# One program per engine for two stages of a diffusion block, with the heads' buffers laid over the front stage's

## The chip, the core and the metric

The kernel runs on one core of one Trainium2 chip. A core has four compute engines, TensorE (PE, matrix products), VectorE (DVE), ScalarE (ACT) and GpSimd (POOL), and a sync engine (SP) that here only issues DMAs. Each engine runs its own list of instructions, and they meet only through semaphores. The metric is the device time of one execution in microseconds (us).

## The reference, cut to what matters

One layer (DEPTH is 1) of a diffusion backbone over 2048 latent tokens and 256 context tokens of width 1024:

```python
shift, scale, gate = split(silu(c) @ w_ada + b_ada, 3)            # also from c_ctx for the context tokens
hc = rmsnorm(ctx) * (1 + scale_c) + shift_c                       # (256, 1024)
hx = rmsnorm(x + sincos) * (1 + scale) + shift                    # (2048, 1024)
s_f, s_b = final_state(hc @ w_in[:, :3072])                       # one 128x128 state per head and direction
i_in, z_f, z_b, q_in, gate_a, u_f, gate_f = split(hx @ w_in)      # 7 pieces of 1024 columns
k = (1 - lb) * sigmoid(-z);  log_f = log(max(1 - k, 1e-6))        # 8 heads of 128, forward and backward
o = chunk_scan(silu(q), k_f, v, log_f, s_f) + flip(chunk_scan(...backward...))
y_a = rmsnorm_per_head(o) * silu(gate_a)
y_f = (real 2-D Fourier mix of u_f, 4 groups) @ w_fourier * silu(gate_f)
out = rmsnorm(x + gate * (concat(y_a, y_f) @ w_out))
```

## The kernel before

Three stages follow each other, each a function: `front`, `heads` and `tail`. Products are made in three passes, of high and low parts of both factors (`mm3`, L60 to L62), so each product costs three matmuls.

**front** (0 to 617 us) makes the hidden rows and holds them in SBUF as 4 groups of 512 tokens (`h_hi`, `h_lo`). It then multiplies them with blocks of 256 weight columns: the value columns (kind 0, four blocks) and the columns of `gate_a` (kind 1, four blocks), eight fills of 256 tokens each (`rows_fill`), which ScalarE evacuates and stores to DRAM. Among the fills stand, for each head, `context_forget` (forget gates of the context), `turn_key` and `context_state`; VectorE's `weigh` lies between the first two. `residual_gate(j)` makes a quarter of the row `gate`. Last comes head 0: `context_forget(0)` and the 12 products `first_unit`, which give head 0 its keys (forward, backward) and its query, since the heads stage computes these only for the next head. Each weight block is loaded to `raw` by SyncE and split by VectorE in `split_block`; `HOME` says in which of two homes the parts lie, `block_a(n)` and `block_c(h)` give the number of the block of gate columns n or of head h's forget columns.

**heads** (617 to 1985 us) runs 8 heads of 4 steps. A step (L987 on) takes 512 tokens in both directions: TensorE makes the scores level by level, VectorE prepares the next step's operands (`prepare`, `first_operands`), and between these TensorE computes ten half products (`project_half`) of 12 matmuls for columns that the next head or the tail needs. Their weights come from GpSimd's DMA into `head_raw`, are split by ScalarE (high part, L1064) and VectorE (low part, L1126).

**tail** (1991 us to the end) does the Fourier mix, the output product and the last norm.

What sets the order is the program text of each stage. Every stage is a `nc.Block()` of its own: it starts when all engines have met at a barrier and ends with another. Its buffers and semaphores belong to a `Room`. When a room is left, a further block in which only GpSimd works clears the room's semaphores one by one (L100), and `heads` has one more block before it, `start_at_one` (L127), that adds one to each of its semaphores but one. GpSimd's list has 72 clears behind front, 32 behind heads and 86 behind tail. Because front's room is closed before heads' is opened, heads' first loads, its memsets and the split of its first weights all come behind front's last store and these blocks.

Of the kernel before, what the change touches and what calls it, by code (L numbers as in the profile page):

```python
# [22 lines left out]

# [11 lines left out]
P = 128  # L35
# [29 lines left out]
def after(n):  # L65

    return n + 1


# [11 lines left out]
class Room:  # L83

    def __init__(self, nc, stage):
        self.nc, self.stage, self.stack, self.sems, self.at_one = nc, stage, ExitStack(), [], []
# [29 lines left out]
    def sem(self, name, from_zero=False):  # L118
        s = self.stack.enter_context(self.nc.semaphore(f"{self.stage}_{name}"))
        self.sems.append(s)  # L120
        if not from_zero:
            self.at_one.append(s)
        return s

    def start_at_one(self):

        with self.nc.Block() as block:  # L127

            @block.gpsimd
            def _(pool):  # L130
                for s in self.at_one:
                    pool.sem_inc(s, 1)


# [18 lines left out]
def front(nc, x_rows, ctx_rows, w_ada, w_in, conds, b_ada, b_ada_cols, norm_w_cols, bounds_cols, row_codes, col_code, masks_in,  # L153
          ident, masks, one_minus_lb, h_base, h_hi, h_lo, states, value_rows, gate_rows_a, pieces, gate_row):

# [9 lines left out]
    BLOCKS = 17  # L165

# [10 lines left out]
    HOME = (0, 1, 0, 0, 1, 1, 0, 0, 1, 1, 0, 0, 1, 1, 0, 0, 1)  # L177

    def fill_of(kind, n, f):
        return (KT + 1) * n + f if kind == 0 else (KT + 1) * NB + KT * n + f  # L180

    FIRST_FILL = (KT + 1) * NB + KT * NB

    def store_of(kind, n, f):
        return KT * (NB * kind + n) + f

    FIRST_STORE = 2 * KT * NB
# [3 lines left out]
    with Room(nc, "front") as r:  # L191
        hc_base = r.slab("hc", 2 * HC)
        hc_hi, hc_lo = r.at("hc_hi", [P, KT, CTX], hc_base, F32R), r.at("hc_lo", [P, KT, CTX], hc_base + HC, F32R)
        work = r.slab("work", 61440)
        raw = r.at("raw", [P, KT, W], work)
# [1065 lines left out]

# [802 lines left out]
```

## Time and profile before

| | us |
|---|---|
| median of 3 runs | 2613.98 (2613.46 to 2616.17) |
| the profiled execution | 2614.39 |
| its span, first to last instruction | 2612.5 |
| TensorE busy | 2472.2 (95% of the span) |
| VectorE busy | 1446.9 (55%) |
| ScalarE busy | 504.9 (19%) |
| mean granted TensorE clock | 0.972 |

The profiled execution is 1.9 us longer than its span, and 0.4 us over the median. Busy time says how much an engine worked; a wait says which event ended its idle time. TensorE is busy for 95% of the span, so what is left between its matmuls is small and lies at few places. Clock 1.00 means 2.4 GHz and 0.50 means 1.2 GHz.

### The profile page before, as it was taken

How to read it: one execution, taken by the hardware profiler on the slowest of the kernel's cores; microseconds unless marked ns; L12 is line 12 of the kernel's file. 1: busy time of each engine (PE TensorE's matmuls, PEld its weight loads, DVE VectorE, ACT ScalarE, POOL GpSimd, SP SyncE). 2: the span in 40 equal slices, each digit the busy share in tenths (PEclk: the TensorE clock that was granted, in tenths of full speed). 3: DMA queues.
4: the chain of work that ended last, by engine and by line, in shares of the span. 5: the costliest groups of instructions: out<-in, count | busy, mean ns of one | idle time of the engine just before them, and what ended most of it. 6: DMA issues, size and time to landing. Idle time of an engine off the chain costs nothing. (4 is left out here: it accounts for less than half of the span.)

```text
span 2612.5 us, 38225 instructions
## 1 busy us (share of the span) xinstructions
PE 2472.2 (95%) x15856; PEld 2134.5 (82%) x15856; DVE 1446.9 (55%) x2984; ACT 504.9 (19%) x775; POOL 44.0 (2%) x64
## 2 busy tenths in 40 slices
PE   7899999995999999999999999999995999799997
PEld 3799999994888888888888888888884787688885
DVE  4712121111676767666666666666785675555553
ACT  3611111110111112111111111111111333222221
POOL 0000000000000000000000000000000001000000
PEclk9899999997999999999999999999997999899999
DMA  8332233213223232323233232323224336344341
GB/s 292 109 91 68 83 97 98 88 53 91 68 86 109 88 101 84 109 79 114 91 104 93 91 106 86 105 88 109 72 89 171 123 148 234 134 157 152 130 175 55
DMA packets 215646, 288.90 MB, mean 111 GB/s; under 512 B 13609, under 2 KB 146865, under 8 KB 211890
## 3 DMA queue, kind: packets, MB, share of 16 engines
q1 hardware_dynamic: 128114, 173.33, 20.1%
q10 hardware_dynamic: 79728, 85.34, 9.4%
q0 software_dynamic: 7632, 27.79, 3.6%
q8 instruction: 126, 2.06, 0.3%
q14 instruction: 46, 0.38, 0.0%
HBM read 193.08 MB, written 93.33 MB: 110 GB/s over the span
## 5 line engine op out<-in xcount | busy, mean ns | idle before, releaser
L60 PE MATMUL head_ps_proj<-hidden_h_hi,head_hi 128*128 128x512 f32 x1184 | 487.9, 412 | 25.4 <-DVE head_lo L1126 25.4
L62 PE MATMUL head_ps_proj<-hidden_h_hi,head_lo 128*128 128x512 f32 x1184 | 465.0, 393 | 0.0
L61 PE MATMUL head_ps_proj<-hidden_h_lo,head_hi 128*128 128x512 f32 x1184 | 463.6, 392 | 0.0
L60 PE MATMUL front_bank<-front_hi,hidden_h_hi 128*128 128x256 f32 x1024 | 294.9, 288 | 6.2 <-DVE hidden_h_lo L364 6.2
L62 PE MATMUL front_bank<-front_hi,hidden_h_lo 128*128 128x256 f32 x1024 | 291.5, 285 | 0.0
L61 PE MATMUL front_bank<-front_lo,hidden_h_hi 128*128 128x256 f32 x1024 | 291.5, 285 | 0.0
L1080 ACT ACTIVATE head_projected<-head_ps_proj 128x512 f32<-128x512 f32 x148 | 88.5, 598 | 1003.1 <-PE head_ps_proj L62 1003.1
L60 PEld LDWEIGHTS head_ps_proj<-hidden_h_hi,head_hi 128*128 128x128 f32 x1184 | 224.3, 189 | 68.0 <-issue 25.7
L62 PEld LDWEIGHTS head_ps_proj<-hidden_h_hi,head_lo 128*128 128x128 f32 x1184 | 223.6, 189 | 50.1
L61 PEld LDWEIGHTS head_ps_proj<-hidden_h_lo,head_hi 128*128 128x128 f32 x1184 | 224.6, 190 | 39.6
L60 PEld LDWEIGHTS front_bank<-front_hi,hidden_h_hi 128*128 128x128 f32 x1024 | 198.4, 194 | 11.4 <-DVE hidden_h_lo L364 9.4
L1209 DVE TENSOR_TENSOR head_query<-head_query,head_total 128x256 f32<-128x256 f32 x256 | 108.4, 423 | 172.5 <-PE head_ps L1011 119.0
L61 PEld LDWEIGHTS front_bank<-front_lo,hidden_h_hi 128*128 128x128 f32 x1024 | 198.4, 194 | 0.0
L62 PEld LDWEIGHTS front_bank<-front_hi,hidden_h_lo 128*128 128x128 f32 x1024 | 198.3, 194 | 0.0
L1171 DVE RECIPROCAL head_inverse<-head_gate 128x448 f32<-128x448 f32 x64 | 186.1, 2932 | 0.0
L1011 PEld LDWEIGHTS head_ps<-head_query,head_key 128*128 128x128 f32 x1024 | 124.9, 193 | 6.6 <-DVE head_key L1210 1.1
L1011 PE MATMUL head_ps<-head_query,head_key 128*128 128x64 f32 x1024 | 122.4, 273 | 1.5 <-DVE head_key L1210 1.0
L1194 DVE TENSOR_TENSOR head_query<-head_query,head_gate 128x512 f32<-128x512 f32 x64 | 44.3, 693 | 142.0 <-PE head_ps L998 142.0
L60 PE MATMUL tail_bank<-tail_w_hi,tail_a_hi 128*128 128x512 f32 x256 | 104.2, 407 | 7.3 <-DVE tail_a_lo L1619 7.3
L1145 DVE COPY_PREDICATED head_score<-hidden_masks,head_ps 128x512 f32<-128x512 uint8 (+1 forms) x192 | 109.1, 621 | 0.0
L1046 PE MATMUL head_ps<-head_value,head_score 128*128 128x128 f32 x512 | 99.6, 276 | 10.0 <-DVE head_state L1240 10.0
L998 PE MATMUL head_ps<-head_query,head_first_half 128*128 128x64 f32 x512 | 100.5, 279 | 7.7 <-DVE head_key L1185 7.7
(213 smaller groups left out, 4322.3 us busy)
## 6 DMA issues: line engine op xcount, KB each, us to landing
head_raw<-in_w_in POOLq DMA_DIRECT2D x37, 512.0 KB, 5.1
head_query<-piece_query SPq DMA_DIRECT2D x64, 256.0 KB, 5.3
head_value<-value_rows SPq DMA_DIRECT2D x64, 256.0 KB, 6.4
head_out<-head_o ACTq DMA_DIRECT2D x64, 256.0 KB, 4.7
tail_o<-head_out SPq DMA_DIRECT2D x32, 512.0 KB, 5.9
front_raw<-in_w_in SPq DMA_DIRECT2D x17, 512.0 KB, 4.7
front_w_mod<-in_w_ada SPq DMA_DIRECT2D x8, 1024.0 KB, 14.0
front_stage<-in_x SPq DMA_DIRECT2D x16, 512.0 KB, 8.5
```

Source lines behind the costliest of these rows:

```text
L60: nc.tensor.matmul(out, st_hi, mv_hi, start=start, stop=False)
L61: nc.tensor.matmul(out, st_hi, mv_lo, start=False, stop=False)
L62: return nc.tensor.matmul(out, st_lo, mv_hi, start=False, stop=stop)
L998: done = nc.tensor.matmul(half_block(ps[d][0][:, t, :], d, half), tile(keys, t), half_block(tile(query[d][b], t), d, half), start=True, st ...
L1011: done = nc.tensor.matmul(meeting(ps[d][BANK_OF[i]][:, t, :], d, LEVELS[i]), tile(key[d][b], t), meeting(tile(query[d][b], t), d, LEVELS[i ...
L1046: nc.tensor.matmul(ps[d][2][:, t, :], score[d][:, t, :], value[d][b][:, t, :], start=True, stop=False)
L1080: nc.scalar.activation(projected[unit % 2][:], ps_proj[unit % 2][:], PIECES[name][1], scale=PIECES[name][2]).then_inc(proj_copied, 1)
L1145: nc.vector.copy_predicated(dst, mask.to_broadcast(list(dst.shape)), src).then_inc(copied[d], 1)
L1171: nc.vector.reciprocal(in_blocks(inverse[d][:], d)[:, :, 1:BASE], in_blocks(gate[d][:], d)[:, :, 1:BASE]).then_inc(gated[d], 1)
L1194: nc.vector.tensor_tensor(qs, qs, f[:, :, 0:1].to_broadcast([P, GRP // BASE, BASE]), ALU.mult)
L1209: nc.vector.tensor_tensor(qs[:, :, 1, :], qs[:, :, 1, :], tot[:, :, 0, :].to_broadcast(shape), ALU.mult)
```

## The change

Front and heads become one block, so that each engine goes on from its last front instruction to its first heads instruction without a barrier; what heads needs is passed as semaphores with counts (`Handover`), and waited for one by one at the first use. The heads' buffers are laid at fixed offsets in front's work area, over buffers that are spent by then, and the eight PSUM banks are shared. The fourth block of gate columns, with its residual gate, moves behind head 0's pieces, and head 7's context work is put between and ahead of these. `start_at_one` goes (a wait for a count of zero is left out instead), and the clears move: front's 72 into heads at head 2, heads' 33 to the beginning of the tail, 40 of the tail's 86 into the tail, with 46 left in a block at the end. No product and no ScalarE or VectorE arithmetic of the steps is changed. VectorE makes one cast more and two memsets fewer, ScalarE one copy and two table loads fewer.

```diff
 class Room:
     def __exit__(self, failed, *a):
-        if self.sems and not failed:
-            with self.nc.Block() as block:
-                @block.gpsimd
-                def _(pool):
-                    for s in self.sems:
-                        pool.sem_clear(s)
         self.stack.close()
+    def clear(self, pool, but=()):
+        kept = [s.num for s in but]
+        for s in self.sems:
+            if s.num not in kept:
+                pool.sem_clear(s)
-    def start_at_one(self):
-        with self.nc.Block() as block:
...
 # front: numbers of the weight blocks, fills and stores
     def block_c(h):
-        return 15 if h == 0 else 2 * h
+        return 14 if h == 0 else 13 if h == 7 else 2 * h
     def block_a(n):
-        return 7 + 2 * n
-    BLOCK_Q = 16
+        return 16 if n == NB - 1 else 7 + 2 * n
+    BLOCK_Q = 15
...
 # front, SyncE
-            for n in range(NB):
+            for n in range(NB - 1):
                 load_block(COL_GA + n * W, block_a(n))
                 load_gate(n)
                 sp.wait_ge(gate_row_done, n + 1)
                 load_forget(NB + n)
                 store_gate(n)
+            load_forget(HEADS - 1)
             load_forget(0)
             sp.wait_ge(lo_done, BLOCK_Q)
             sp.dma_start(raw[:, :, 0:P], w_view[:, :, COL_Q:COL_Q + P]).then_inc(w_here, DMA)
-            sp.wait_ge(gate_out, NB * DMA)
-            sp.wait_ge(masks_in_sem, DMA)
+            load_block(COL_GA + (NB - 1) * W, block_a(NB - 1))
+            load_gate(NB - 1)
+            store_gate(NB - 1)
 # front, VectorE, after the loop over the gate blocks
-            split_block(block_c(0), 28)
-            v.wait_ge(product, fill_of(1, NB - 1, KT - 1) + 1)
-            split_block(BLOCK_Q, 29, P)
+            split_block(block_c(HEADS - 1), 24)
+            v.wait_ge(product, fill_of(1, NB - 2, KT - 1) + 1)
+            split_block(block_c(0), 26)
+            weigh(HEADS - 1)
+            v.wait_ge(z_done, HEADS - 1)
+            split_block(BLOCK_Q, 27, P)
             weigh(0)
+            v.wait_ge(product, FIRST_FILL + 2 * NG)
+            split_block(block_a(NB - 1), 28)
+            add_gate_bias(NB - 1)
 # front, TensorE, after the loop over the gate blocks (ScalarE's list is moved alike)
+            context_forget(HEADS - 1)
+            for unit in range(2):
+                first_unit(block_c(0), 0, unit)
+            turn_key(HEADS - 1)
+            first_unit(block_c(0), 0, 2)
+            context_state(HEADS - 1)
+            first_unit(block_c(0), 0, 3)
             context_forget(0)
-            for unit in range(NG):
-                first_unit(block_c(0), 0, unit)
+            for unit in range(NG, NG + 2):
+                first_unit(block_c(0), P, unit)
             turn_key(0)
-            first_unit(block_c(0), P, NG)
+            first_unit(block_c(0), P, NG + 2)
             context_state(0)
-            for unit in range(NG + 1, 2 * NG):
-                first_unit(block_c(0), P, unit)
+            first_unit(block_c(0), P, NG + 3)
             for unit in range(2 * NG, 3 * NG):
                 first_unit(BLOCK_Q, 0, unit)
+            residual_gate(NB - 1)
+            for f in range(KT):
+                rows_fill(1, NB - 1, f)
 # heads: buffers at fixed places in front's work slab, banks shared with front
-    with Room(nc, "head") as r:
-        raw = r.sb("raw", [P, KT, P])
-        hi = [r.sb(f"hi{b}", [P, KT, P], F32R) for b in range(2)]
+    HC, VALUES, QUERY_W, RAW, GATE_W, OUT_ROWS, LITTLE = (work + i * KB for i in (60, 44, 28, 0, 8, 24, 76))
+    raw = r.at("raw", [P, KT, P], HC)
+    hi = [r.at(f"hi{b}", [P, KT, P], at, F32R) for b, at in enumerate((HC + 2 * row, GATE_W))]
...
+    ps_proj = bank[4:6]
+    ps = [[by_tile[6 + d], by_tile[d], by_tile[2 + d]] for d in range(2)]
 # heads, GpSimd
-                for d in range(2):
-                    pool.memset(score[d][:], 0.0).then_inc(cleared, 1)
-                    pool.memset(first_half[d][:], 0.0).then_inc(cleared, 1)
+        pool.wait_ge(handed.z_done, HEADS)
+        name, head = pieces(0, False)[0]
+        pool.dma_start(raw[:], w_view[:, :, bass.ds(PIECES[name][0] + head * P, P)]).then_inc(w_here, DMA)
+        pool.wait_ge(handed.product, handed.first_fills)
+        for d in range(2):
+            pool.memset(first_half[d][:], 0.0).then_inc(near_cleared, 1)
+        pool.wait_ge(handed.product, handed.all_fills)
+        pool.wait_ge(handed.gate_out, N_BLOCKS * DMA)
+        for d in range(2):
+            pool.memset(score[d][:], 0.0).then_inc(score_cleared, 1)
+        turn(0, False, first=1)
...
+            if h == 2:
+                for d in range(2):
+                    pool.wait_ge(product[d], PROD * NG * h)
+                    pool.wait_ge(o_stored[d], NG * h * DMA)
+                front_room.clear(pool)
 # heads, SyncE
+        def first_loads():
+            for o_stage in range(2):
+                sp.wait_ge(handed.stored[o_stage], handed.keys_stored)
+            sp.wait_ge(handed.z_done, HEADS)
+            sp.wait_ge(handed.s_done, HEADS)
+            load(0, 0, ("key", "value"))
+            for o_stage in range(2):
+                sp.wait_ge(handed.stored[o_stage], handed.queries_stored)
+            sp.wait_ge(handed.s_out, HEADS * 2 * DMA)
+            load(0, 0, ("query",))
+            sp.wait_ge(handed.product, handed.first_fills)
+            start_state(0)
+            sp.wait_ge(handed.gate_row_done, N_BLOCKS)
+            load(0, 1, ("key", "query"))
+            sp.wait_ge(handed.product, handed.all_fills)
+            load(0, 1, ("value",))
 # heads, TensorE
+            if n == 0:
+                pe.wait_ge(handed.evacuated, handed.all_fills)
...
-                pe.wait_ge(cleared, 7)
+        pe.wait_ge(handed.sig_done, HEADS)
+        pe.wait_ge(handed.gate_added, N_BLOCKS)
+        pe.wait_ge(handed.key_t_copied, HEADS)
+        pe.wait_ge(handed.s_copied, HEADS)
 # heads, VectorE
-                for d in range(2):
-                    nc.vector.memset(ps[d][2][:], 0.0).then_inc(cleared, 1)
-                v.wait_ge(cleared, 7)
+        v.wait_ge(w_here, DMA)
+        nc.vector.tensor_copy(hi[0][:], raw[:]).then_inc(hi_done, 1)
         split_low(0, 0)
+        v.wait_ge(handed.s_done, HEADS)
         for part in range(GATED + 1):
             prepare(0, 0, part)
+        v.wait_ge(near_cleared, 2)
         first_operands(0, 0)
 # tail, GpSimd, and after its block
                 pool.memset(eps[:], EPS).then_inc(eps_set, 1)
+                heads_room.clear(pool)
...
+                pool.wait_ge(out_stored[1], 2 * DMA)
+                r.clear(pool, but=LATE)
+        with nc.Block() as block:
+            @block.gpsimd
+            def _(pool):
+                for sem in LATE:
+                    pool.sem_clear(sem)
 # program
-            front(nc, x[0], ctx[0], w_ada, w_in, conds, b_ada, b_ada_cols, norm_w_cols, bounds_cols, row_codes, col_code, masks_in,
-            heads(nc, w_in, one_minus_lb, ident, masks, h_hi, h_lo, states, value_rows, pieces, o_rows)
...
+            work = s.slab("work", WORK)
+            bank = [s.ps(f"bank{i}") for i in range(8)]
+            with nc.Block() as block:
+                handed = front(nc, block, front_room, work, bank, x[0], ctx[0], w_ada, w_in, conds, b_ada, b_ada_cols, norm_w_cols,
...
+                heads(nc, block, heads_room, front_room, work, bank, handed, w_in, one_minus_lb, ident, masks, h_hi, h_lo, states,
```

TensorE at the passage from front to heads, before (`front_bank` is a front product, `head_ps_proj` the first half product of heads):

```order
L60 MATMUL front_bank<-hidden_h_hi_52,front_hi_61 128x512
L61 MATMUL front_bank<-hidden_h_lo_56,front_hi_61 128x512
L62 MATMUL front_bank<-hidden_h_hi_52,front_lo_63 128x512
L264 UNCONDITIONAL_BRANCH
L963 UNCONDITIONAL_BRANCH [waits barrier_Pool_Activation_PE_DVE_SP_release]
L60 MATMUL head_ps_proj<-hidden_h_hi_49,head_hi 128x512 [waits head_proj_copied,head_lo_done,head_cleared]
```

The same place in the changed kernel (the products ahead are now of the last gate columns, 256 wide):

```order
L61 MATMUL hidden_bank<-front_hi_61,hidden_h_hi_52 128x256
L62 MATMUL hidden_bank<-front_lo_63,hidden_h_hi_52 128x256
L63 MATMUL hidden_bank<-front_hi_61,hidden_h_lo_56 128x256
L1040 UNCONDITIONAL_BRANCH
L61 MATMUL hidden_bank<-hidden_h_hi_49,head_hi_5978 128x512 [waits front_s_copied,front_key_t_copied,head_lo_done,front_gate_added,front_sig_done]
```

The barrier is gone; the first product of heads waits for the split of its weights and for four front events that lie eight fills back.

VectorE at the same passage, before (the first two rows end `weigh(0)`):

```order
L401 TENSOR_TENSOR front_key<-front_key,front_gate 128x255 [waits front_scan_done]
L402 TENSOR_TENSOR front_key<-front_key,front_gate 128x255
L264 UNCONDITIONAL_BRANCH
L1121 UNCONDITIONAL_BRANCH [waits barrier_Pool_Activation_PE_DVE_SP_release]
L1252 MEMSET head_ps 128x512 x2
L1126 TENSOR_TENSOR head_lo<-head_raw,head_hi 128x1024 [waits head_hi_done,head_cleared]
L1153 TENSOR_SCALAR head_key<-head_key,hidden_one_minus_lb 128x512 [waits head_loaded00]
```

and in the changed kernel:

```order
L406 TENSOR_TENSOR front_key<-front_key,front_gate 128x255
L384 CAST front_hi_61<-front_raw 128x2048 [waits front_w_here,front_product]
L386 TENSOR_TENSOR front_lo_63<-front_raw,front_hi_61 128x2048 [waits front_hi_done]
L411 TENSOR_TENSOR front_gate_part<-hidden_bank,front_gate_part 1x256 [waits front_gate_bias_in,front_gate_row_done]
L1205 UNCONDITIONAL_BRANCH
L1339 CAST head_hi_5978<-head_raw 128x1024 [waits head_w_here]
L1210 TENSOR_TENSOR head_lo_5980<-head_raw,head_hi_5978 128x1024 [waits head_hi_done]
L1237 TENSOR_SCALAR head_key_5988<-head_key_5988,hidden_one_minus_lb 128x512 [waits head_loaded00,front_s_done]
```

The split of the last gate block and the gate's bias stand ahead of the passage now, and the heads' first split and `prepare` follow them with no barrier.

GpSimd's list from front's end on, before (ISA rows are semaphore clears):

```order
L264 UNCONDITIONAL_BRANCH
L97 UNCONDITIONAL_BRANCH [waits barrier_Pool_Activation_PE_DVE_SP_gather]
L100 ISA x72
L95 UNCONDITIONAL_BRANCH
L129 UNCONDITIONAL_BRANCH [waits barrier_Pool_Activation_PE_DVE_SP_gather]
L127 UNCONDITIONAL_BRANCH
L912 UNCONDITIONAL_BRANCH [waits barrier_Pool_Activation_PE_DVE_SP_gather]
L915 MEMSET head_score 128x512
L916 MEMSET head_first_half 128x512
L915 MEMSET head_score 128x512
L916 MEMSET head_first_half 128x512
L921 DMA head_raw<-in_w_in 128x8x128 [waits head_lo_done] x37
```

and in the changed kernel:

```order
L952 UNCONDITIONAL_BRANCH
L961 DMA head_raw<-in_w_in 128x8x128 [waits front_z_done]
L964 MEMSET head_first_half_6000 128x512 [waits front_product]
L964 MEMSET head_first_half_6001 128x512
L968 MEMSET head_score_6008 128x512 [waits front_gate_out,front_product]
L968 MEMSET head_score_6009 128x512
L957 DMA head_raw<-in_w_in 128x8x128 [waits head_lo_done] x14
L93 ISA [waits head_product1,head_o_stored1,head_o_stored0,head_product0]
L93 ISA x71
L957 DMA head_raw<-in_w_in 128x8x128 [waits head_lo_done] x22
```

The 72 clears stand between two weight loads of the heads now, and the first weight load waits for front's last `context_forget` alone.

## Rows read from the trace of the kernel before

**Rows 1.** The longest waits, whole span: engine and line, releaser, total us, times, longest

```profile
PE head_ps_proj L60 <- DVE head_lo L1126: 25.4, 1, 25.4
PE tail_bank L1879 <- DMA tail_chan<-in_chan_tables: 11.5, 1, 11.5
```

**Rows 2.** Timeline, TensorE, front's end to step 1: start us, us, line, tiles, count

```profile
617.11 0.39 PE L62 MATMUL front_bank<-hidden_h_hi,front_lo 128*128 128x512 f32 x1
642.85 0.76 PE L60 MATMUL head_ps_proj<-hidden_h_hi,head_hi 128*128 128x512 f32 x1 [25.35 <-DVE head_lo L1126]
...
654.43 0.66 PE L998 MATMUL head_ps<-head_query,head_first_half 128*128 128x64 f32 x2 [6.13 <-DVE head_key L1185]
...
699.75 0.48 PE L60 MATMUL head_ps_proj<-hidden_h_hi,head_hi 128*128 128x512 f32 x1
```

**Rows 3.** Timeline, TensorE, starts of steps 0 and 1 of head 1

```profile
829.04 0.50 PE L60 MATMUL head_ps_proj<-hidden_h_hi,head_hi 128*128 128x512 f32 x1
...
871.75 0.48 PE L60 MATMUL head_ps_proj<-hidden_h_hi,head_hi 128*128 128x512 f32 x1
```

**Rows 4.** Windows: from:to, us, busy PE, PEld, DVE, ACT, POOL, then PEclk, DMA share

```profile
617.50:642.80 25.30, 0.00 (x0) 0.00 (x0) 2.24 (x4) 1.65 (x2) 2.90 (x5) 0.58 0.52 150
642.80:660.00 17.20, 11.02 (x38) 9.39 (x39) 14.57 (x29) 0.00 (x0) 0.96 (x1) 0.60 0.17 46
...
828.90:871.60 42.70, 42.70 (x289) 36.96 (x288) 32.30 (x86) 8.56 (x12) 1.76 (x2) 1.00 0.34 105
```

**Rows 5.** Timeline, the other engines between front and step 0

```profile
612.10 0.60 ACT L540 ACTIVATE front_out<-front_bank 128x512 f32<-128x512 f32 x1 [4.84 <-PE front_bank L62]
...
617.54 0.60 ACT L540 ACTIVATE front_out<-front_bank 128x512 f32<-128x512 f32 x1 [4.84 <-PE front_bank L62]
618.16 0.33 ACTq L542 DMA_DIRECT2D piece_query<-front_out  x1
...
629.39 0.53 POOL L915 MEMSET head_score<- 128x512 f32 x1 [627.93 <-POOLq L127]
...
641.53 1.22 DVE L1126 TENSOR_TENSOR head_lo<-head_raw,head_hi 128x1024 fp32r<-128x1024 f32 x1 [10.93 <-ACT head_hi L1064]
```

**Rows 6.** DMA by issue line and queue, 617 to 643 us: count, KB, us to landing

```profile
q14 instruction: 1, 0.01, 0.1%
...
head_value<-value_rows SPq DMA_DIRECT2D x4, 256.0 KB, 8.5
...
piece_query<-front_out ACTq DMA_DIRECT2D x1, 256.0 KB, 2.4
```

**Rows 7.** Timeline, TensorE and VectorE, work that is moved in front

```profile
431.18 3.62 PE L711 MATMUL front_bank<-front_raw,front_silu 128*2 128x256 f32 x16
...
457.86 0.28 PE L60 MATMUL front_bank<-front_hc_hi,front_hi 128*128 128x256 f32 x1
...
463.62 0.28 PE L60 MATMUL front_bank<-front_hi,hidden_h_hi 128*128 128x256 f32 x1
...
464.45 0.62 DVE L390 TENSOR_SCALAR front_key<-front_key,hidden_one_minus_lb 128x256 f32<-128x256 f32 x2 [20.53 <-ACT front_key L548]
...
469.27 2.29 DVE L382 TENSOR_TENSOR front_lo<-front_raw,front_hi 128x2048 fp32r<-128x2048 f32 x1
...
487.09 1.06 PE L703 MATMUL front_bank<-front_v_ctx,front_key_t 128*128 128x128 f32 x8
```

**Rows 8.** Timeline, the last stores of heads and tail, and tail's start

```profile
1984.61 0.99 ACTq L1105 DMA_DIRECT2D head_out<-head_o  x2
1991.13 0.40 ACTq L1797 DMA_DIRECT2D tail_hn<-in_hgrn_cols  x1
...
2603.10 0.34 ACTq L1795 DMA_DIRECT2D out<-tail_x  x1
```

**Rows 9.** DMA by issue line, around these two stores

```profile
head_out<-head_o ACTq DMA_DIRECT2D x2, 256.0 KB, 2.5
...
out<-tail_x ACTq DMA_DIRECT2D x1, 512.0 KB, 2.6
```

More of the change, by code:

```diff
@@ L22 @@
 from contextlib import ExitStack
+from dataclasses import dataclass
 import concourse.bass as bass
@@ L150, with front @@
 N_BLOCKS = HG // W
-def front(nc, x_rows, ctx_rows, w_ada, w_in, conds, b_ada, b_ada_cols, norm_w_cols, bounds_cols, row_codes, col_code, masks_in,
+KB = 1024
+WORK = 78 * KB
+@dataclass
+class Handover:
+    z_done: object
+    sig_done: object
+    key_t_copied: object
+    s_done: object
+    s_copied: object
+    s_out: object
+    gate_row_done: object
+    gate_added: object
+    gate_out: object
+    product: object
+    evacuated: object
+    stored: list
+    masks_in: object
+    first_fills: int
+    all_fills: int
+    keys_stored: int
+    queries_stored: int
+    all_stored: int
+def front(nc, block, r, work, bank, x_rows, ctx_rows, w_ada, w_in, conds, b_ada, b_ada_cols, norm_w_cols, bounds_cols, row_codes, col_code, masks_in,
           ident, masks, one_minus_lb, h_base, h_hi, h_lo, states, value_rows, gate_rows_a, pieces, gate_row):
@@ new lines, in front @@
+    stage0 = [r.at(f"stage{b}", [P, D], work + 28672 + 4096 * b) for b in range(4)]
+    TMP = 3
+    tmp = [r.at(f"tmp{i}", [P, GRP], work + 45056 + 2048 * i) for i in range(TMP)]
+    col = r.at("col", [P, H], work + 51200)
+    junk = r.at("junk", [P, D], work + 53248)
+    v_ctx = r.at("v_ctx", [P, CT, HG], work + 45056)
+    key = r.at("key", [P, 2, CTX], work + 53248)
+    gate = r.at("gate", [P, 2, CTX], work + 55296)
+    key_t = r.at("key_t", [P, 2, CT, P], work + 57344)
+    state = r.at("state", [P, 2, P], work + 59392)
@@ new lines, in heads @@
+    inverse = [piece(f"inverse{d}", VALUES + (4 + d) * row) for d in range(2)]
+    first_half = [piece(f"first_half{d}", QUERY_W + (1 + d) * row) for d in range(2)]
+    key_t = [tiles(f"key_t{d}", QUERY_W + (3 + d) * row) for d in range(2)]
+    state = [r.at(f"state{d}", [P, TPG + 1, P], QUERY_W + 5 * row + d * (TPG + 1) * P * 4) for d in range(2)]
+    total = [r.at(f"total{d}", [P, 2 * GRP // BASE], QUERY_W + 15 * KB + d * KB // 2) for d in range(2)]
+    score = [tiles(f"score{d}", at) for d, at in enumerate((GATE_W + 7 * row, LITTLE))]
@@ L1296, in tail @@
     H = D // 2
-    KB = 1024
     F_FIRST = 6
@@ L2007, in program @@
     y_f = scratch("fourier_out", (FW, SEQ))
-    with Room(nc, "all") as r:
+    with Room(nc, "all") as r, Room(nc, "head") as heads_room:
         ident = r.sb("ident", [P, P])
-        with Room(nc, "hidden") as s:
+        with Room(nc, "hidden") as s, Room(nc, "front") as front_room:
             masks = s.sb("masks", [P, 2, MASKED, P], U8)
```

1869 lines of the change are left out of this document (935 added, 934 removed).

## The prediction, made before the changed kernel was run

> **What bounds the kernel now.** I read the busy shares first: TensorE 95%, VectorE 55%. So TensorE bounds the kernel, and only what stands between its matmuls, or slows them, can be won. The list of waits comes next. The longest single idle time of TensorE is the passage from front to heads, 25.4 us, and after it the start of the tail, 11.5 us [rows 1]. The chain of waits says nothing on the first: it is followed back only to 1991 us, where all engines leave a barrier together. So the timeline and the windows must carry the argument.
>
> The timeline shows the whole price of the passage [rows 2]. The last front matmul starts at 617.11 us; matmuls of this shape follow each other at 0.23 us, so without the passage the next would start at 617.34. The first of heads starts at 642.85: 25.51 us lost. Step 0 then runs until step 1 starts at 699.75, which is 56.90 us. The same step of head 1, with the same work, takes from 829.04 to 871.75, 42.71 us [rows 3]. So step 0 loses 14.19 us more. Of these, 6.13 are a wait for VectorE's first operands [rows 2]; the other 8.06 go to the clock. After the idle time the granted clock is 0.60 in the window of 17 us in which step 0 begins, while it is 1.00 in the undisturbed step [rows 4]; 0.50 is the lower level, 1.2 GHz.
>
> The other engines' timeline says what the 25 us consist of [rows 5]. ScalarE's last store is issued at 618.16 and lands 2.4 us later [rows 6], at 620.56. The first heads instructions start at 629.39, after 72 clears, 31 increments and three barriers. Then GpSimd's weights, ScalarE's split and VectorE's split (641.53) follow one after another, all with TensorE idle.
>
> **Part 1: the passage.** TensorE's work is the same: the eight fills of the last gate block and one residual gate go behind the twelve products of head 0, and context work of head 7 goes ahead. If nobody makes TensorE wait, front still ends at 617.34 and step 0 follows at once, 42.71 us long. Whether it waits is a matter of when the others are ready, so I place them on before's times.
>
> Eight fills are 384 matmuls at 0.12 us (48 matmuls from 457.86 to 463.62 are 5.76 us [rows 7]), 46.1 us, and the residual gate takes 3.6 [rows 7]. So head 0's query is done at 617.3 - 46.1 - 3.6 = 567.6, and its keys four products of 5.44 us [rows 5] earlier, at 545.9.
> - VectorE splits the gate block after the keys (a cast of about 1.2 us, then 2.29 [rows 7]): 549.4. The residual gate's weights may then be loaded; even at the 8.5 us of the slowest load in the passage [rows 6] they are there at 558, before 567.6.
> - VectorE adds the gate's bias at about 571.6. SyncE stores it, and then issues the keys and values of step 0, and the queries, whose store was issued at about 568.2 and has landed by 571. With six issues of about 0.5 us and 8.5 us to land [rows 6], all is there by 583.
> - VectorE's path from its first split to the first operands is 641.53 to 654.43, 12.9 us [rows 2, 5], at its own pace, since it waits there for no matmul. Its cast in ScalarE's place adds about 1 us. So operands stand at 597, when TensorE still has 20 us of fills. The low part of the weights is ready at 574.
> - GpSimd clears `first_half` at 568 and `score` from 617.3 on, two memsets of 0.53 us [rows 5]. VectorE first uses `score` only after step 0's first scores, some 8 us into the step.
> - The values of step 1 wait for the last fill too: 617.3 + 8.5 = 626; in head 1, VectorE takes up the next step's keys 15 us into the step.
>
> Further ahead, the tightest place is where the forget columns of head 0 are split. VectorE must wait for the end of gate block 2 (487.09 [rows 7]) and needs 3.5 us: 490.6. TensorE meanwhile does a context state, 1.06 us, and `context_forget(7)`, 5.76 us [rows 7], and wants them at 493.9. The margin is 3.3 us. `weigh(7)` and `weigh(0)` have two products, 10.9 us, as cover; VectorE takes from 464.45 to about 468.0 for one, the cast of a block ahead of 469.27 taken off [rows 7], so 3.6 us.
>
> The branch that is left on TensorE between the stages has no row. Its cost lies between 0 and what two barriers with their branches cost, 1.4 us (worked out below); I take 0, since the branches in before sit inside those barriers. The page Runtime: NRT & Kernel Launch of the Trainium skill (Instruction fetch mechanics) warns that a taken branch whose target is not yet fetched stalls the engine for a fetch; by the time of a small DMA that would add about 2 us. The trace speaks against it here: from 617 to 643 us, with two such branches on each engine, the view of the queues lists one instruction packet in all [rows 6].
>
> Part 1 saves 25.51 + 14.19 = 39.70 us. Bounds: if all idle time and slow clock goes, 39.7; if only the barriers and clears go (629.39 - 620.56), 8.8.
>
> **Part 2: clears and barriers elsewhere.** Clears have no rows, but three stretches hold them. Behind heads: the second store is issued about 0.6 us after 1984.61 and lands 2.5 us later, at 1987.7; the tail starts at 1991.13 [rows 8, 9]. That is 3.4 us for 32 clears and two barriers. Behind the tail: issued at 2603.10, landed after 2.6 us at 2605.7, end of the span 2612.5, so 6.8 us for 86 clears and two barriers [rows 8, 9]. The difference, 3.4 us for 54 clears, gives 0.062 us for one and 1.4 us for two barriers. The third stretch tests it: 103 x 0.062 + 3 x 0.7 = 8.5 us, where 8.8 were measured.
> - Behind heads 32 clears and one barrier go: 2.0 + 0.7 = 2.7 us. The 33 clears lie at the tail's beginning on GpSimd, whose first other work there comes after the folds, far later. Bounds 0 and 3.4.
> - At the end 40 clears go: 2.5 us. They run inside the tail, where GpSimd is done. Bounds 0 and 6.8.
> - Front's 72 clears in head 2 hold GpSimd for 4.5 us between two weight loads. Those weights are used a good part of a head later. Cost nothing; without that cover 4.5 us.
> - The tail's first wait, 11.5 us, gets shorter by the 2.7 us already counted, and stays over 8 us, so I leave the lower clock behind it as it is.
>
> **The sum.** 39.7 + 2.7 + 2.5 = 44.9 us, from 2614.39 gives 2569.5. The profiled execution is 0.4 over the median of the runs, less than I can tell, so 2569.5 stands for the median too.
>
> **Rivals.**
> - A new wait at the passage. VectorE's or SyncE's chain comes over 20 us later than I place it, for instance because SyncE, blocked at the gate's bias, issues the loads late and one wait of 5 us opens before the first scores. Then the clock falls as well and costs up to the 8.1 us above: 2569.5 + 5 + 8 = 2582.5. For it: every one of these loads now stands behind the gate's store in SyncE's list. Against: 20 us of slack, on durations that the trace has.
> - A small hole, up to 3 us, at the split of head 0's columns (3.3 us of margin), or a stalled branch: 2572. By the skill's rule above it would be 2571.5, which is this rival too.
> - Clears and barriers don't get cheaper, since the landing of the last store and a fixed time behind it set both ends: 2614.4 - 39.7 = 2574.7. For it: no row shows a clear. Against: three stretches fit one price.
> - The change doesn't do what it says: TensorE's first heads product still waits for something that comes at the very end of front, and only the 8.8 us of barriers are saved there: 2614.4 - 8.8 - 5.2 = 2600.4.
> - Slower. In every step of the heads, a buffer or bank that now has another place makes TensorE wait for VectorE, where before the two were just in time. VectorE is busy 32.3 of 42.7 us in a step [rows 4], so some 10 us of lag must be used up at one point. With 32 steps it decides from 44.9 / 32 = 1.4 us a step on; at 1.6 us a step the kernel takes 2569.5 + 51 = 2620.7. Against: no instruction or wait of a step is changed but for the first.
>
> **How the numbers follow.** My forecast 0.74, with 2567 to 2572.5 as its own range; the small hole 0.07; clears at their old price 0.05; new wait 0.08; nothing hidden 0.03; slower 0.02; about as before, from a mixture of the last two, 0.01. What a measurement can tell from no change is 0.2%, 5.2 us. All but the last two cases lie more than that below before: faster 0.97, same 0.01, slower 0.02. The range runs from 2565, for steps that gain a little at the tail's start, to 2579, which takes in the small hole, the clears, and the shorter new waits.
>
> **What would show it.** In the changed profile: TensorE's longest wait at the passage under 1 us; granted clock 1.00 through it; step 0 about 42.7 us; front's last matmul at 617 us still, with no wait of TensorE between 480 and 617; VectorE idle for some 20 us before step 0's first scores; the tail's first DMA about 2.7 us sooner after the last heads store; the span ending about 4.3 us after the last store lands instead of 6.8; the steps of later heads as long as before. A wait of TensorE for `head_lo` or `head_key`, a window with a clock under 1.00 around 620 us, or a longer step would prove me wrong.

## The result, and the profile after

The changed kernel takes 2566.51 us (median of 4 runs, 2565.05 to 2569.57), the kernel before 2613.72 (4 runs, 2612.65 to 2616.17). The ratio is 0.982, with an interval from 0.9803 to 0.9837: 47.2 us less. The forecast was 2569.5, in a range from 2565 to 2579. The span of the profiled execution is 2563.3 us, 49.2 less than before.

The timeline of TensorE in the changed kernel shows the passage from front to heads (columns as in [rows 2]):

```profile
615.08 0.28 PE L63 MATMUL hidden_bank<-front_hi,hidden_h_lo 128*128 128x256 f32 x1
615.20 0.40 PE L61 MATMUL hidden_bank<-hidden_h_hi,head_hi 128*128 128x512 f32 x1
...
657.75 0.48 PE L61 MATMUL hidden_bank<-hidden_h_hi,head_hi 128*128 128x512 f32 x1
```

The last product of front and the first of heads are 0.12 us apart, where [rows 2] have 25.74. Step 0 lasts from 615.20 to 657.75, 42.55 us, where it was 56.90. The windows that answer to [rows 4] have TensorE busy throughout, at the full clock:

```profile
617.50:642.80 25.30, 25.30 (x185) 21.70 (x184) 17.26 (x48) 2.85 (x4) 0.88 (x1) 1.00 0.31 97
642.80:660.00 17.20, 17.20 (x106) 15.24 (x105) 11.72 (x26) 5.70 (x8) 0.00 (x0) 1.00 0.13 38
```

The other engines' timeline answers to [rows 5]. The rows of VectorE and SyncE say how early step 0 was ready:

```profile
565.63 0.98 POOL L964 MEMSET head_first_half<- 128x512 f32 x2 [43.63 <-PE hidden_bank L63]
...
569.14 0.41 DVE L411 TENSOR_TENSOR front_gate_part<-hidden_bank,front_gate_part 1x256 f32<-1x256 f32 x1 [21.75 <-PE hidden_bank L726]
...
569.58 0.24 SPq L309 DMA_DIRECT2D residual_gate<-front_gate_part  x1
570.00 0.36 SPq L992 DMA_DIRECT2D head_key<-piece_key_f  x1
...
590.10 0.42 DVE L1269 TENSOR_TENSOR head_key<-head_key,head_inverse 128x256 f32<-128x256 f32 x1
...
619.88 0.69 DVE L1278 TENSOR_TENSOR head_query<-head_query,head_gate 128x512 f32<-128x512 f32 x1 [29.35 <-PE hidden_bank L1075]
```

SyncE issues the first heads load at 570.00, behind the gate's store. The first operands stand at 590.5. TensorE asks for them at 617.95, so 27 us were in hand. VectorE then sits idle for 29.35 us until the first scores: slack that was on TensorE before is on VectorE now, where it costs nothing.

The two other borders, which answer to [rows 8], are the last store of heads with the tail's first instruction, and the last store of all (the span ends at 2563.3):

```profile
1940.38 0.99 ACTq L1190 DMA_DIRECT2D head_out<-head_o  x2
1944.09 0.40 ACTq L1884 DMA_DIRECT2D tail_hn<-in_hgrn_cols  x1
...
2556.66 0.34 ACTq L1882 DMA_DIRECT2D out<-tail_x  x1
```

The first distance falls from 6.52 to 3.71 us, the second (2603.10 to 2612.5 before) from 9.40 to 6.64. Of TensorE's longest waits the one for `head_lo` is gone, and the one for the tail's channel tables is shorter (line, releaser, total us, times, longest; 11.5 before [rows 1]):

```profile
PE tail_bank L61 <- DVE tail_fold_lo L1628: 11.1, 1, 11.1
...
PE tail_bank L1966 <- DMA tail_chan<-in_chan_tables: 8.1, 1, 8.1
...
PE tail_bank L1975 <- DVE tail_once L1618: 6.0, 1, 6.0
```

So the span's 49.2 us come from the passage (39.86), the border behind heads (2.81), the end (2.76), and 3.8 us that no part of the change aims at. About 2.1 of these lie in front's first 130 us, and 2.2 at the start of the last head; the tail, from its first instruction to its last store, is 0.6 us longer. From the start of step 1 of head 0 to the first scores of the last head both kernels take 1162.9 us. At the start of the last head both kernels wait 1.58 us for VectorE ahead of the first scores. Before, the clock falls behind this wait; in the changed kernel it doesn't (before first, then changed: the wait, then a window over the end of these scores):

```profile
1862.70 0.41 PE L998 MATMUL head_ps<-head_query,head_first_half 128*128 128x64 f32 x2 [1.58 <-DVE head_key L1185]
...
1866.00:1870.00 4.00, 4.00 (x17) 0.50 1.01 328
```

```profile
1820.69 0.41 PE L1075 MATMUL hidden_bank<-head_query,head_first_half 128*128 128x64 f32 x2 [1.58 <-DVE head_key L1269]
...
1824.00:1828.00 4.00, 4.00 (x25) 1.00 1.05 349
```

Both differences are looked at behind the experiments.

### The profile page after: what moved, and what is told of

The parts are those of the page before. It is cut to its first block and busy times, and to the rows that moved or that the text cites. A ratio compares the mean times of both kernels' runs of the same rounds, so it can differ in the third digit from the quotient of the medians.

```text
span 2563.3 us, 38144 instructions
## 1 busy us (share of the span) xinstructions
PE 2461.8 (96%) x15856; PEld 2126.8 (83%) x15856; DVE 1447.1 (56%) x2983; ACT 501.2 (20%) x772; POOL 44.0 (2%) x64
## 5 line engine op out<-in xcount | busy, mean ns | idle before, releaser
L61 PE MATMUL hidden_bank<-hidden_h_hi,head_hi 128*128 128x512 f32 x1184 | 485.3, 410 | 0.0
L63 PE MATMUL hidden_bank<-hidden_h_hi,head_lo 128*128 128x512 f32 x1184 | 463.0, 391 | 0.0
L62 PE MATMUL hidden_bank<-hidden_h_lo,head_hi 128*128 128x512 f32 x1184 | 461.3, 390 | 0.0
L61 PE MATMUL hidden_bank<-front_hi,hidden_h_hi 128*128 128x256 f32 x1024 | 294.8, 288 | 6.2 <-DVE hidden_h_lo L368 6.2
L62 PE MATMUL hidden_bank<-front_lo,hidden_h_hi 128*128 128x256 f32 x1024 | 291.5, 285 | 0.0
L63 PE MATMUL hidden_bank<-front_hi,hidden_h_lo 128*128 128x256 f32 x1024 | 291.5, 285 | 0.0
L63 PEld LDWEIGHTS hidden_bank<-hidden_h_hi,head_lo 128*128 128x128 f32 x1184 | 222.2, 188 | 49.6
L61 PEld LDWEIGHTS hidden_bank<-hidden_h_hi,head_hi 128*128 128x128 f32 x1184 | 222.8, 188 | 41.8
L62 PEld LDWEIGHTS hidden_bank<-hidden_h_lo,head_hi 128*128 128x128 f32 x1184 | 223.2, 188 | 39.2
L61 PEld LDWEIGHTS hidden_bank<-front_hi,hidden_h_hi 128*128 128x128 f32 x1024 | 198.4, 194 | 11.4 <-DVE hidden_h_lo L368 9.4
```

The lines of the kernel that those rows point to most:

```text
L61: nc.tensor.matmul(out, st_hi, mv_hi, start=start, stop=False)
L62: nc.tensor.matmul(out, st_hi, mv_lo, start=False, stop=False)
L63: return nc.tensor.matmul(out, st_lo, mv_hi, start=False, stop=stop)
```

## Experiments

Theory: TensorE loses nothing at a border as long as every other engine can run over it ahead of TensorE. That needs two things at once: no barrier at the border, and TensorE work at front's end that doesn't feed step 0. Rivals: only the barriers and clears were dear, or only the order was; or the low clock has a cause of its own. Each kernel is the changed one with the edit shown, but for one, which starts from the kernel before. Its ratio is against the kernel before on the same chip.

### Two blocks

```diff
+            with nc.Block() as block:
                 heads(nc, block, heads_room, front_room, ...
```

> The changed kernel, but heads stand in a block of their own, so that the engines meet at a barrier between front and heads; the new order of the front, the buffers and the moved clears stay. My theory (the passage is gained because the engines run on over the border, so that head 0's loads, splits and first operands are made under the front's last products): TensorE is idle again for about 25.5 - 8 (104 clears and increments and their barriers are gone) = 17.5 us at the border, waits again for the second half of the operands (6.1) and runs step 0 at the low clock (8.1): 2566.5 + 31.7 = about 2598. Rival A (the order alone brings the gain, the border costs a barrier of 0.7 us): 2567 to 2569. Rival B (the low clock doesn't come back after a shorter gap): 2590.

Measured: 2594.75 us, 0.9932 [0.9917, 0.9947], 28.2 over the changed kernel. TensorE's waits between 600 and 660 us:

```profile
PE hidden_bank L61 <- DVE head_lo L1210: 11.7, 1, 11.7
PE hidden_bank L1075 <- DVE head_key L1269: 7.1, 1, 7.1
```

One line of code brings back 28 of the 47 us, so rival A falls, and rival B with it. Step 0 runs from 627.54 to 684.66, 57.12 us: 7.1 are the second wait and 7.5 the clock. The gap alone is smaller than I expected, 11.8 us against 17.5. GpSimd's first load is issued at 617.85, 2.3 us after the last front product, where the kernel before without its clears, below, needs 5.8. Of these 3.5 us some 2.0 lie at the barrier, and the rest in memsets that stand ahead of the load there. I read the first part as the barrier having less to wait for when front's last work doesn't feed heads; no run tests it alone.

### The old order in one program

```diff
-        for n in range(NB - 1):
+        for n in range(NB):
             residual_gate(n)
...
-        residual_gate(NB - 1)
-        for f in range(KT):
-            rows_fill(1, NB - 1, f)
```

(and the same on the other engines: head 0's query comes last again)

> The changed kernel as one program per engine, but with the kernel before's order in the front: the last gate columns' 8 fills stand ahead of head 0's pieces again, which come last. My theory: with the query's pieces last, their evacuation, store, load and split for step 0 can't lie beside TensorE's work: idle for about 20 us at the border, and then step 0 at the low clock (8 us more): 2566.5 + 28 = about 2595. Rival A (the barrier and the clears were the whole cost, the order does nothing): 2566 to 2569. Rival B (the gap comes back but the clock stays): 2587.

Measured: 2588.84 us, 0.9911 [0.9894, 0.9928], 22.3 more. The wait at the passage is now:

```profile
PE hidden_bank L1048 <- DVE head_key L1242: 16.9, 1, 16.9
```

TensorE goes from its last front product (616.82) straight into the first projection of heads (617.05), since its weights are long there, and then waits 16.88 us for operands made from queries that were just stored. Step 0 takes 63.80 us, 21.25 over the undisturbed one: 16.88 of wait and 4.4 of clock. Rival A falls here too. My 28 was too much, on both terms: the first projection covers part of the wait, and the clock came back sooner. VectorE's first instruction of heads shows what it waited for:

```profile
625.12 0.49 DVE L1210 TENSOR_SCALAR head_key<-head_key,hidden_one_minus_lb 128x512 f32<-128x512 f32 x1 [67.74 <-DMA head_query<-piece_query]
```

The keys were loaded from 598.50 on, and VectorE's work from here to 635.04 reads keys and not queries, but `loaded` counts both loads in one semaphore. With a semaphore for the keys alone the old order might lose less; that wasn't run, so the 21.3 below hold for this kernel's semaphores.

### The kernel before without its clears at the border

```diff
-                    for s in self.sems:
-                        pool.sem_clear(s)
...
-        r.start_at_one()
...
+                    if h == 2:
+                        front_room.clear(pool)
```

> The kernel before, with its order and its blocks, but without the work between front and heads: the front's 72 clears are made in head 2, and the increments that let the heads' counts start at one are gone (the waits for zero are left out instead). One clear more stands in a block of its own at the end (0.8 us). My theory: 104 clears and increments at 0.062 and two barriers go from the border, 8.1 us; the gap shrinks from 25.5 to 17.4, and step 0 is still at the low clock: 2613.7 - 8.1 + 0.8 = 2606.4. Rival A (the clears lie beside something else): 2614. Rival B (a shorter gap leaves the clock at the full level): 2598.

Measured: 2604.84 us (median of 7, 2599.29 to 2608.85), 0.9966 [0.9955, 0.9977]: 8.9 less than before. The timeline of TensorE at the passage:

```profile
635.78 0.76 PE L60 MATMUL head_ps_proj<-hidden_h_hi,head_hi 128*128 128x512 f32 x1 [16.76 <-DVE head_lo L1137]
...
647.33 0.66 PE L1009 MATMUL head_ps<-head_query,head_first_half 128*128 128x64 f32 x2 [6.08 <-DVE head_key L1196]
```

The gap is 8.6 us shorter (16.76 against 25.35 [rows 2]), as 72 clears, 31 increments and two barriers should make it. The wait behind it is the same, and step 0 (to 692.45) loses 8.0 to the clock as before, so rivals A and B both fall.

Together these four kernels give what TensorE loses at the passage, as the gap and the excess of step 0 over 42.55 us:

| | a barrier at the border | one program |
|---|---|---|
| old order | 31.0 (39.9 with the clears) | 21.3 |
| new order | 26.4 | 0 |

Each half alone brings 4.6 or 9.7 of the 31.0 us. The rest comes only when both are there. The 31.0 are of the kernel before with its own buffers and lists, so the 4.6 holds what these bring as well.

### Gaps of chosen length

```diff
+        pool.wait_ge(lo_done, 1)
+        pool.dma_start(...).then_inc(w_here, DMA)
+        for _ in range(160):
+            pool.sem_clear(spare)
+        pool.sem_inc(hold, 1)
...
         pe.wait_ge(handed.s_copied, HEADS)
+        pe.wait_ge(hold, 1)
```

(0 clears in the short hold, 60 in the middle one, 160 in the long one)

> The changed kernel, but GpSimd issues its second load early and TensorE waits at the start of the heads for an increment of GpSimd's that follows; everything else is ready by then. My theory: a gap of about 2 us, step 0 at the full clock: 2566.5 + 2 = 2568.5. Rival (any gap at this place brings the low clock): 2 + 8 = 2576.

> As the short hold, but with 160 clears of a spare semaphore (0.062 us each, 9.9 us) ahead of the increment that TensorE waits for. My theory: a gap of about 12 us, with everything else ready, after which step 0 is at the low clock for part of its length: 2566.5 + 12 + 4 to 8 = 2582 to 2587. Rival A (the low clock comes from the start of a new block or of heads as such, not from the idle time): 2578.5. Rival B (waiting engines catch up in the gap and the heads lose less than the gap): under 2576.

> As the short and the long hold, with 60 clears of the spare semaphore (0.073 us each by the run with 460 more): a gap of about 4.9 us. In the other gaps the granted clock fell 5 to 6 us after TensorE's last product. My theory: the clock stays at the full level and the time is 2566.5 + 4.9 = 2571.4. Rival (the clock falls in this gap too): step 0 is longer by 1.5 us (as after the long hold) to 8 us (as before the change), 2573 to 2579.

Measured: short 2566.81 (0.9824 [0.9809, 0.9838]), middle 2576.51 (0.9859 [0.9844, 0.9874]), long 2583.18 (0.9887 [0.9872, 0.9901]). The short hold made a gap of only 0.7 us, too little to tell anything but that 0.7 us here leave the clock alone. The other two, as TensorE's waits show them, the middle one first and the long one second:

```profile
PE hidden_bank L61 <- POOLq L974: 5.1, 1, 5.1
```

```profile
PE hidden_bank L61 <- POOLq L974: 12.2, 1, 12.2
```

Windows of TensorE around the middle gap (from:to, us, busy and matmuls, granted clock, DMA share, GB/s):

```profile
622.00:624.00 2.00, 0.00 (x0) 1.00 1.06 312
624.00:626.00 2.00, 1.15 (x3) 0.73 0.68 227
626.00:628.00 2.00, 2.00 (x6) 0.50 0.00 0
628.00:630.00 2.00, 2.00 (x14) 0.92 0.00 0
```

Step 0 is 44.22 us long behind the middle gap and 44.10 behind the long one: 1.7 and 1.6 over the undisturbed step. So the low level does come behind idle time alone, with no new block and nothing late, and a gap of 5.1 us is enough here: the clock is still 1.00 from 622 to 624 and falls as TensorE goes on (624.85). My expectation for the middle hold, that the clock stays, was wrong; its rival holds, at its lower end. So was 4 to 8 us for the long one: the clock was back after some 3 us of work. The 8 us of the kernel before are reached only where a second wait follows in step 0: 7.5 (two blocks), 8.0 (without clears) and 8.2 (before), against 1.6, 1.7 and 4.4 with one gap. But the place of the wait matters too. Behind the holds TensorE goes on with the first projection, and the clock is back in 3.2 and 3.5 us. In the old order in one program the one wait lies ahead of the first scores; TensorE goes on with these, and the clock is back only after 8.8 us, which is the 4.4. With another wait first, the clock is back 11.0 to 12.0 us after the wait ahead of the scores. So one wait at that place already accounts for some half of the 8 us; no run has two waits elsewhere, so the share of the second wait as such isn't shown. In the two-block kernel the windows show both falls:

```profile
626.00:628.00 2.00, 0.46 (x1) 0.50 1.08 367
...
630.00:632.00 2.00, 1.99 (x8) 0.84 1.20 317
632.00:634.00 2.00, 0.00 (x0) 1.00 0.49 140
634.00:636.00 2.00, 0.00 (x0) 0.51 0.01 4
...
648.00:650.00 2.00, 2.00 (x6) 0.50 0.00 0
650.00:652.00 2.00, 2.00 (x8) 0.72 0.00 0
```

The clock rises during the first projection, falls again in the second wait, and stays low until about 651.

The medians rose by 10.0 and 16.7, more than the 6.8 and 13.8 of the passage. In both profiled runs the last head is 2.2 us longer, with the clock low behind its first wait as in the kernel before, and front is longer in its first 130 us: its last product starts at 619.44 and 618.78 instead of 615.08.

### More clears, and fewer at the end

```diff
-                for sem in LATE:
-                    pool.sem_clear(sem)
+                for _ in range(11):
+                    for sem in LATE:
+                        pool.sem_clear(sem)
...
+                for _ in range(6):
                     front_room.clear(pool)
```

> The changed kernel, but the 46 clears at the end are made 11 times over (460 more) and the front's 72 clears in head 2 six times over (360 more, 22 us of GpSimd). My theory: 460 x 0.062 = 28.5 us more at the end, nothing in head 2, where GpSimd has only loads to issue: 2566.5 + 28.5 = 2595. Rival A (clears cost nothing beside the last store): 2566.5. Rival B (GpSimd's clears in head 2 delay a load that the next head waits for): up to 22 more, 2617.

Measured: 2599.93 us, 0.9956 [0.9939, 0.9973], 33.4 more. The last store is issued at 2556.50, as in the changed kernel, and the span ends at 2596.9: the stretch grows from 6.64 to 40.40 us, 33.76 for 460 clears, 0.073 each. My 0.062 was a sixth too low. The 360 clears more in head 2 cost nothing. GpSimd's weight loads around them:

```profile
1077.36 0.89 POOL L957 DMA_DIRECT2D head_raw<-in_w_in  x1 [39.67 <-DVE head_lo L1211]
1131.49 0.88 POOL L957 DMA_DIRECT2D head_raw<-in_w_in  x1 [53.24 <-DVE head_lo L1211]
```

They stand 54.13 us apart, as in the changed kernel (1077.13 and 1131.26), with GpSimd in clears for some 30 us of it. So rivals A and B both fall.

```diff
                 r.clear(pool, but=LATE)
+                pool.wait_ge(a_lo_done, NT)
+                for sem in MIDDLE:
+                    pool.sem_clear(sem)
...
-                for sem in LATE:
+                for sem in LAST:
                     pool.sem_clear(sem)
```

> The changed kernel, but 17 of the 46 clears at the end are made by GpSimd after the last split of the head rows, while TensorE still multiplies; 29 are left at the end. My theory (the clears at the end cost 0.062 us each and nothing else stands there): the stretch from the last store's issue to the end of the span falls from 6.64 to 5.6 us, 1.05 us less; the time 2565.5. Rival (the store's landing ends the span, the clears lie beside it): the stretch stays at 6.6.

> The changed kernel again, for the comparison with the early clears on the same chip: 2566.5, within 0.1%.

Measured: 2566.36 (0.9823 [0.9808, 0.9838]) beside 2567.61 for the changed kernel again (0.9826 [0.9811, 0.9841]). The two times can't be told apart. The profile can: the last store is issued at 2557.71, the span ends at 2563.1, so the stretch is 5.39 us instead of 6.57 in the changed kernel's second profile (2556.93 to 2563.5). That is 1.2 us for 17 clears, 0.07 each, the same price.

### The same idea at the next border

```diff
+        sp.wait_ge(proj_done, 20 * (HEADS - 1) + NG * len(OF_THIS))
+        early_loads(sp)
...
-                load_u(0)
-                load_table(0)
...
-                split_cw_low(0)
                 fold(0)
+                split_cw_low(0)
```

(`early_loads` loads the tail's first wave rows and its four tables over the hidden rows; the second of the two kernels leaves `split_cw_low(0)` where it was)

> The changed kernel, and the same idea at the next border: the tail's first wave rows (2 MB) and its four tables are loaded during the last head's last step, when nothing reads the hidden rows they are laid over, and VectorE folds the wave rows ahead of splitting the channel weights. In the changed kernel's trace the fold begins at 1956.15, when the rows have landed and both splits are done, and TensorE waits 5.98 and 11.11 us for what comes of it; the tail's first instruction is at 1944.09. My theory: the fold begins at 1944.3 and VectorE's last split of this group ends at about 1963.5 instead of 1973.7: 10 us less, 2556.5. Rival A (the early load delays the last step's own work, or the fold waits for the channel weights' splits on ScalarE anyway): 2562 to 2567. Rival B (TensorE gets the same pause later, since the tables' splits come next): 2561.

> The same early loads, but VectorE's order stays: the splits of the channel weights first, then the fold. These splits end at 1956.24 in the changed kernel's trace, as the rows land. My theory: the loads alone bring next to nothing, 0 to 2 us (2565 to 2567), since the instruction ahead of the fold on VectorE is as late as the transfer. Rival (the transfer is what all wait for): 2556.

Measured: 2556.44 us with both edits, 0.9783 [0.9768, 0.9797], which is faster than both kernels; 2567.07 us with the loads alone, 0.9827 [0.981, 0.9843], on the same chip. VectorE and TensorE at the tail's start with both edits:

```profile
1914.41 0.37 SPq L2110 DMA_DIRECT2D all_early_u<-piece_wave  x1
```

```profile
1946.71 2.29 DVE L1615 TENSOR_TENSOR tail_once<-all_early_u 128x2046 f32<-128x2046 f32 x1
...
1965.96 0.55 PE L61 MATMUL tail_bank<-tail_cw_hi,tail_fold_hi 128*128 128x256 f32 x1 [6.26 <-DVE tail_fold_lo L1627]
```

And with the loads alone:

```profile
1953.99 0.69 DVE L1637 TENSOR_TENSOR tail_cw_lo<-tail_bank,tail_cw_hi 128x512 fp32r<-128x512 f32 x1 [9.21 <-ACT tail_cw_hi L1825]
...
1956.19 0.69 DVE L1637 TENSOR_TENSOR tail_cw_lo<-tail_bank,tail_cw_hi 128x512 fp32r<-128x512 f32 x1 [1.51 <-ACT tail_cw_hi L1825]
1956.80 2.28 DVE L1615 TENSOR_TENSOR tail_once<-all_early_u 128x2046 f32<-128x2046 f32 x1
```

With the loads alone the data is there, and VectorE still sits 9.21 us in front of a split that it can't make yet, with the fold queued behind it. With the order changed too, the first product of the wave rows starts 19.45 us after the tail's first instruction (1946.51), instead of 29.75 (1944.09 to 1973.84): 10.3 us less, and the median is 10.1 lower. As at the passage, one half alone brought next to nothing. The other half, the new order without the early loads, wasn't run. Both expectations take the wave rows to land at about 1956 in the changed kernel; its trace has their load issued at 1945.04 and landed 8.4 us later, at about 1953.4, while the fold starts at 1956.15. So the order alone may bring some 2.7 us, an estimate from these three numbers.

## Why the prediction was right

| term | predicted | measured |
|---|---|---|
| idle time at the passage | 25.51 | 25.51 (no idle time is left) |
| second wait and clock in step 0 | 14.19 | 14.35 (56.90 to 42.55) |
| behind heads | 2.7 | 2.81 |
| end of the kernel | 2.5 | 2.76 |
| sum | 44.9 | 45.4; medians 47.2 |

- **Passage.** Each time that I placed was near: query products done at 565.5 (placed 567.6), gate bias from 569.1 (571.6), loads from 570.0, operands at 590.5 (597). The slack was larger than I said, 27 instead of 20 us. The margin of 3.3 us at the split of head 0's columns held: TensorE has no wait at all between 480 and 660 us. The new-wait rival and the small hole did not come.
- **The branch.** I took 0 for the branch between the stages, though the Trainium skill, Runtime: NRT & Kernel Launch (Instruction fetch mechanics), states that a taken branch whose target hasn't been fetched stalls the engine. TensorE's two products around it start 0.12 us apart, as any two of that shape. No run here shows the stall; whether the target had been fetched by then, the trace doesn't say.
- **Clears.** The mechanism was right, and a clear costs 0.073 us instead of 0.062. The 40 at the end are then worth 2.9 instead of 2.5. At 0.073 the two stretches that I took the price from leave 1.1 and 0.5 us for their two barriers, not 1.4 for both, so my price for a barrier was too high, and no run measures it alone. The rival by which clears don't matter is refuted by the run with 460 more of them.
- **The clock.** The term was right for this kernel, since I took it from this kernel's own step. But I treated the 8 us as the price of a gap of this length. The holds show that one gap ahead of the first projection costs 1.6 or 1.7 us; the rest was lost behind the second wait, ahead of the scores. Had a new wait of 5 us opened ahead of the scores, as in my rival, it would more likely have cost some 9 us in all than 13. That is an estimate, 5 plus the 4.4 of the old order in one program; no run has it.
- **What is left.** The time came out 3.0 us below the forecast, and 0.5 us below the 2567 that I gave as the lower end of my main case. About 2 us of the medians' 47.2 are no term of mine; I had nothing for them, and that the range held them was partly luck. It reached down to 2565 for a gain at the tail's start, and the tail is 0.6 us longer instead. The profiles show two places.

  The first is the start of the last head. In the kernel before, the two blocks, the kernel before without clears and the middle and long holds, the clock falls there and the last head is 2.1 to 3.7 us longer; in the changed kernel's two profiles and the six others it stays. The five are those with a gap of 5 us or more ahead of the first heads product. With this the medians fit: 45.4 + 2.2 is 47.6, where 47.2 were measured; 26.4 + 2.1 is 28.5 for the two blocks (28.2), and the holds come to 9.0 and 16.0 (10.0 and 16.7). Why a gap at 620 us should matter at 1820 isn't shown by any run.

  The second is front's first 130 us. In the ten profiles of kernels with the new order front is the same, and its last product starts between 615.08 (the changed kernel) and 619.44 (the middle hold). The profiles part in the first 24 us, in how long TensorE waits for its first modulation weights (9.9 us in all in the changed kernel, 11.3 in the middle hold), and then in how soon the clock comes back after each pause. A late window of the stretch, first the changed kernel, then the middle hold:

```profile
120.00:128.00 8.00, 8.00 (x65) 0.94 0.00 0
```

```profile
120.00:128.00 8.00, 6.89 (x38) 0.59 0.00 0
```

What decides this in a given kernel stays open; each kernel has one profile, or two, and no run here separates chance from the kernel's layout.

## What to carry to other kernels

At a border between stages, look at what stands last before it on each engine, not only at the barrier. The bounding engine runs through only if it has work there that the next stage doesn't need, and if the others may pass it: either alone brings a small part. The same holds for a prefetch, which is worth nothing while the instruction that uses it is queued behind a later one. A gap's price is its length plus the clock, and the clock's part depends on what follows: 1.6 or 1.7 us behind one gap ahead of a projection, 4.4 behind one ahead of the scores, 7.5 to 8.2 with a gap at both places. Where a profile has such a gap, compare the later stages too before you put the whole difference down to it: here 2.2 us of it lay 1200 us further on.

## What the runs showed of the hardware

- A semaphore clear on GpSimd costs 0.073 us (33.76 us for 460), and an otherwise unused GpSimd hides 432 of them inside a head.
- The granted clock was 0.50 behind a gap of 5.1 us, and the step behind it was 1.7 us longer. Behind 12.2 us at the same place it was 1.6, so here the loss didn't grow with the gap.
- Behind a wait of 16.88 us ahead of the scores it took 8.8 us to come back and 4.4 us were lost.
- At the start of the last head, behind the same wait of 1.58 us, it fell in five of thirteen profiles and stayed in eight.
- With two waits in a row (11.7 and 7.1 us) the clock rose between them, fell again, and the loss was 7.5 us.
